# Attention scores from split float32r parts, and outputs gated where they are turned, in a two-layer hybrid block

## The reference, cut to what matters

```python
proj = h @ w_in[l]
q_a, kv_c, kv_s, kv_w, g_nsa, z_a, q_b, kv_b, z_b, merge = jnp.split(proj, pts, axis=-1)
kc = compress_blocks(...)                       # 31 compressed tokens
o_cmp, p_cmp = compressed_attention(qa, kc, vc, slopes_a)
o_slc = selected_attention(qa, ks, vs, blk_idx, slopes_a)
o_win = banded_attention(qa, kw, vw, slopes_a, NSA_WINDOW)       # 512
o_a = gts[0] * o_cmp + gts[1] * o_slc + gts[2] * o_win
y_a = (merge_heads(o_a) * jax.nn.silu(z_a)) @ w_o_nsa[l]
o_b = banded_attention(qb, kb, vb, slopes_b, SWA_WINDOW, sinks=sinks[l])   # 128
y_b = (merge_heads(o_b) * jax.nn.silu(z_b)) @ w_o_swa[l]
# in each of them: s = einsum(q, k) * dh ** -0.5, ALiBi, softmax, einsum(p, v); dh = 64
y = (jax.nn.sigmoid(m_a) * y_a + jax.nn.sigmoid(m_b) * y_b) @ w_out[l]
```

## Time and profile before

| | |
|---|---|
| runs | 1763.94, 1768.17, 1769.01 us; median 1768.17 |
| profiled execution | 1767.28 us, its span 1765.6 us |
| instructions | 28455 |
| busy | PE 95%, PE weight loads 86%, DVE 43%, POOL 34%, ACT 31% of the span |
| chain that ended last | issue 40%, PE 38%, POOL 17%, DVE 4%, ACT 1% |
| DMA | 141 MB, 80 GB/s on average |
| mean granted TensorE clock | 0.969 |

### The profile page before, as it was taken

The page is one execution under the profiler, slowest core; times in us unless marked ns, Lnnn a source line. Parts: engine busy times, 40 slices in busy tenths (PEclk is TensorE's granted clock), DMA queues, the critical chain, the costliest instruction groups (busy, mean ns, idle before and its releaser), DMA issues.

```text
span 1765.6 us, 28455 instructions
## 1 busy us (share of the span) xinstructions
PE 1668.9 (95%) x11374; PEld 1520.6 (86%) x11374; DVE 764.2 (43%) x1617; ACT 541.4 (31%) x870; POOL 605.7 (34%) x485
## 2 busy tenths in 40 slices
PE   5898999999989999999999999899999999999996
PEld 5676777777767799999999999899899899998996
DVE  5705555555566743323333311424622632371355
ACT  2323333333333432233322222323332242232222
POOL 3453222221225324444333444232442243233323
PEclk9999999999999889999999999899999999999998
DMA  8132111111124212222222222121121122212111
GB/s 323 72 120 83 46 40 46 47 48 48 48 96 167 96 49 95 95 75 92 74 92 95 95 76 92 49 75 69 64 81 72 49 73 72 72 50 74 70 49 72
DMA packets 22774, 141.15 MB, mean 80 GB/s; under 512 B 3248, under 2 KB 3248, under 8 KB 6448
## 3 DMA queue, kind: packets, MB, share of 16 engines
q1 hardware_dynamic: 18752, 131.08, 20.6%
q10 hardware_dynamic: 3952, 9.00, 1.4%
HBM read 137.98 MB, written 2.10 MB: 79 GB/s over the span
## 4 chain that ended last, share of the span: by engine, by line
issue 40%; PE 38%; POOL 17%; DVE 4%; ACT 1%; POOLq 0%; DVEq 0%; ACTq 0%
PE lin L365 31%; POOL w_lo L311 17%; PE aux L789 4%; PE aux L754 2%; DVE mix L1472 1%; PE aux L738 1%; PE aux L436 1%; DVE squares L1491 0%; DVE v_T L1492 0%; PE aux L393 0%; DVE residual L1511 0%; DVE tmp L1407 0%; PE aux L711 0%; PE aux L741 0%; ACT mix L1024 0%
## 5 line engine op out<-in xcount | busy, mean ns | idle before, releaser
L311 POOL TENSOR_TENSOR w_lo<-w_raw,w_hi 128x512 fp32r<-128x512 f32 x460 | 601.9, 1340 | 1141.8 <-ACT w_hi L353 1141.8
L365 PE MATMUL lin<-x_hi,w_hi 128*128 128x256 f32 (+2 forms) x2448 | 595.5, 311 | 32.7 <-POOL w_lo L311 16.9
L365 PE MATMUL lin<-x_lo,w_hi 128*128 128x256 f32 (+2 forms) x2448 | 584.1, 307 | 0.0
L365 PE MATMUL lin<-x_hi,w_lo 128*128 128x256 f32 (+2 forms) x2448 | 582.8, 306 | 0.0
L365 PEld LDWEIGHTS lin<-x_hi,w_hi 128*128 128x128 f32 x2448 | 396.9, 192 | 66.2 <-issue 24.5
L365 PEld LDWEIGHTS lin<-x_hi,w_lo 128*128 128x128 f32 x2448 | 396.7, 191 | 18.8
L365 PEld LDWEIGHTS lin<-x_lo,w_hi 128*128 128x128 f32 x2448 | 396.7, 191 | 14.8
L353 ACT ACTIVATE w_hi<-w_raw 128x2048 fp32r<-128x2048 f32 x115 | 219.4, 1908 | 158.1 <-PE lin L365 152.6
L861 ACT ACTIVATE prob<-prob,neg_max 128x31 f32<-128x31 f32 (+6 forms) x128 | 60.1, 471 | 157.5 <-DVE neg_max L1201 157.5
L1322 DVE TENSOR_TENSOR conv_in<-conv_c_gate,lin 128x272 f32<-128x272 f32 (+1 forms) x32 | 12.3, 427 | 213.8 <-PE lin L365 213.8
L365 PE MATMUL lin<-mix,w_hi 128*128 128x272 f32 (+1 forms) x512 | 84.7, 287 | 10.0 <-DVE mix L1472 7.1
(11 more groups left out here) (294 smaller groups left out, 2005.4 us busy)
## 6 DMA issues: line engine op xcount, KB each, us to landing
w_raw<-wstream SPq DMA_DIRECT2D x115, 1024.0 KB, 4.8
ada_shift_scale<-w_ada SPq DMA_DIRECT2D x8, 1024.0 KB, 19.0
ada_gate<-w_ada_gate ACTq DMA_DIRECT2D x4, 1024.0 KB, 5.9
residual<-x_t SPq DMA_DIRECT2D x1, 2048.0 KB, 8.7
residual<-x_t ACTq DMA_DIRECT2D x1, 2048.0 KB, 8.4
out_t<-residual ACTq DMA_DIRECT2D x8, 256.0 KB, 2.1
small_inputs<-smalls ACTq DMA_DIRECT2D x1, 537.0 KB, 3.4
residual<-meta_t ACTq DMA_DIRECT2D x1, 64.0 KB, 11.1
```

Of the source, the lines that this page charges most:

```text
L311: ins = eng.tensor_tensor(wlo[h][:, cols], raw[h][:, cols], whi[h][:, cols].bitcast(F32), ALU.subtract)
L365: ins = t.matmul(o, w[half][:, c0:c0 + P], x(k, t0, cnt), start=(n == 0), stop=(n == 3 * kts - 1))
```

## The change

Keys and queries are kept as a high float32r part and a low rest. The high keys lie twice, once on each half of the lanes, for each head; a head's queries lie with the high part on its own 64 lanes and the low part on the other 64. A score product is then two float32r matmuls: over 128 lanes, both parts of the queries by the high keys; and over 64 lanes, high queries by low keys. The compressed keys get a 32nd column of zeros. ACT writes the high parts (keys: four copies of 64 lanes; queries: two), DVE the low ones (two of 64 lanes). The scores of the next pair's first step go ahead of the last turn of a pair. The turned outputs are multiplied by z at once, in place in `zz`; behind the loop only the split is left, in an order that leaves the last pair to the end, and the first chunk's four tiles run together, input block by input block, two of them in other banks.

The core of the diff:

```diff
-        K_C, V_C, K_S, V_S, K_W, V_W, Q_B, K_B, V_B = 4, 5, 6, 7, 8, 9, 10, 14, 15
+        V_S, V_W, V_B = range(3)
+        K_S, K_W, K_B = range(3)
...
-            with eng.bass.Fori(0, NPAIR, 1, engines=[eng.engine]) as ii:
-                def scores(s):
...
-                    qa = proj[lo:hi, K_C, P * i:P * i + P]
-                    qb = proj[lo:hi, V_C, P * i:P * i + P]
-                    eng.matmul(b[0][:, 0:keys], qa, proj[lo:hi, K_S, 0:keys], start=True, stop=True)
-                    eng.matmul(b[1][:, 0:keys], qa, proj[lo:hi, K_W, 0:keys], start=True, stop=True)
-                    eng.matmul(b[2][:, 0:NC], qa, kct[lo:hi, e * NC:(e + 1) * NC], start=True, stop=True)
-                    w0 = 32 + (P if i == 0 else 0)
-                    eng.matmul(b[2][:, w0:w0 + keys - k0], qb, proj[lo:hi, K_B, k0:keys], start=True,
-                               stop=True).then_inc(s_scored, 1)
-
+            def scores(s, ii):
+                i, e = divmod(s, 2)
+                lo, hi = PAIR[e]
+                b = att_banks(e)
+                keys, k0 = P * (i + 1), max(0, P * (i - 1))
+                eng.wait_ge(s_o, ii * 8 + (s - 1 + CREDIT))
+                if e == 0:
+                    eng.wait_ge(s_oT_out, ii * 4 + (i - 1 + CREDIT))
+                if s == 0:
+                    eng.wait_ge(s_q, ii * 2 + 2)
+                if s == 1:
+                    eng.wait_ge(s_oT_out, ii * 4 + CREDIT)
+                qs = slice(P * i, P * i + P)
+                w0 = 32 + (P if i == 0 else 0)
+                for out, x, twice, low in (
+                        (b[0][:, 0:keys], 0, k_hi[:, K_S, e, 0:keys], k_lo[lo:hi, K_S, 0:keys]),
+                        (b[1][:, 0:keys], 0, k_hi[:, K_W, e, 0:keys], k_lo[lo:hi, K_W, 0:keys]),
+                        (b[2][:, 0:NC + 1], 0, kct_hi[:, e, :], kct_lo[lo:hi, e, :]),
+                        (b[2][:, w0:w0 + keys - k0], 1, k_hi[:, K_B, e, k0:keys], k_lo[lo:hi, K_B, k0:keys])):
+                    eng.matmul(out, q_parts[:, x, e, qs], twice, start=True, stop=False)
+                    ins = eng.matmul(out, q_parts[lo:hi, x, e, qs], low, start=False, stop=True)
+                ins.then_inc(s_scored, 1)
+
+            def pair(ii, last):
...
+                if not last:
+                    scores(0, ii + 1)
                 turn_outputs(QT - 1)
 
-            eng.wait_ge(s_tile_out, 6 * NPAIR + CREDIT)
-            for c in range(N_WO):
+            scores(0, 0)
+            with eng.bass.Fori(0, NPAIR - 1, 1, engines=[eng.engine]) as ii:
+                pair(ii, False)
+            pair(NPAIR - 1, True)
+
+            eng.wait_ge(s_tile_out, 4 * NPAIR)
+            eng.wait_ge(s_q, 2 * NPAIR + 2)
+            def wo_tile(c, m, x, ks=None):
+                return group(eng, c % 2, x * 1024 + m * P, 256, 4, [(wo_bank(2 * c + m, x)[:], TB1[0])],
+                             lambda k, t0, n: x_hi(4 * x + k, t0, n), lambda k, t0, n: x_lo(4 * x + k, t0, n), ks)
+
+            chunk_ready(START["wo"])
+            for n, k in enumerate(OG_ORDER):
+                eng.wait_ge(s_og_lo, n + 1)
+                for m in range(2):
+                    ins = wo_tile(0, m, k // 4, ks=[k % 4])
+                    if k % 4 == 3:
+                        ins.then_inc(s_chunk if m and k == KD - 1 else s_wo, 1)
+            for c in range(1, N_WO):
                 chunk_ready(START["wo"] + c)
                 for m in range(2):
                     for x in range(2):
                         j = 4 * c + 2 * m + x
-                        if j >= 2:
+                        if c > 1 or m:
                             eng.wait_ge(s_wo_out, j - 1)
-                        ins = group(eng, c % 2, x * 1024 + m * P, 256, 4, lin_outs(x, TB1),
-                                    lambda k, t0, n, x=x: x_hi(4 * x + k, t0, n), lambda k, t0, n, x=x: x_lo(4 * x + k, t0, n),
-                                    before=(lambda k, x=x: eng.wait_ge(s_og_lo, 4 * x + k + 1)) if j < 2 else None)
-                        ins.then_inc(s_chunk if m and x else s_wo, 1)
+                        else:
+                            eng.wait_ge(s_wo_out, x + 1)
+                        wo_tile(c, m, x).then_inc(s_chunk if m and x else s_wo, 1)
...
+            def query_high_parts(g):
+                for e, (p0, p1) in enumerate(PAIR):
+                    ins = act(q_parts[p0:p1, g, e, :], lin[g][p0:p1, 0, :], ACT.Copy, scale=DH ** -0.5)
+                ins.then_inc(s_qhi, 1)
+
             for c in range(N_PROJ):
                 chunk_lands_and_splits(eng, START["proj"] + c + 1)
                 if c in (1, 2):
                     eng.wait_ge(s_cin, c)
                     act(cin_hi[c - 1][:], cin[:], ACT.Copy).then_inc(s_cin_hi, 1)
+                if c in KEYS:
+                    eng.wait_ge(s_proj, PROJ_ORDER.index(c) + 1)
+                    for e, (p0, p1) in enumerate(PAIR):
+                        for half in range(2):
+                            ins = act(k_hi[half * DH:(half + 1) * DH, KEYS[c], e, :], lin[0][p0:p1, 0, :], ACT.Copy)
+                    ins.then_inc(s_khi, 1)
                 if c == 6:
-                    eng.wait_ge(s_cin, 2)
                     for g in range(2):
                         if g == 0:
                             eng.wait_ge(s_proj, 4)
                         else:
                             eng.wait_ge(s_chunk, START["proj"] + 6)
-                        act(proj[:, Q_HEADS + g, :], lin[g][:, 0, 0:T1], ACT.Copy, scale=DH ** -0.5).then_inc(s_q, 1)
+                        query_high_parts(g)
...
-            for k in range(KD):
-                eng.wait_ge(s_og, k + 1)
-                act(xhi[:, k, 0:T1], tmp[:, k % 2, 0:T1], ACT.Copy).then_inc(s_og_hi, 1)
+            eng.wait_ge(s_chunk, START["wo"])
+            for k in OG_ORDER:
+                x, pr = divmod(k, NPAIR)
+                eng.wait_ge(s_oT_out, 4 * (NPAIR if pr == NPAIR - 1 else NPAIR - 1) + CREDIT)
+                act(xhi[:, k, 0:T1], zz[:, x, pr, :], ACT.Copy).then_inc(s_og_hi, 1)
...
-                    copy(proj[:, CHUNK_TILE[c] + g, :], lin[g][:, 0, :]).then_inc(s_proj_out, 1)
+                    if g == 0 and c in KEYS:
+                        eng.wait_ge(s_khi, KEYS[c] + 1)
+                        for e, (p0, p1) in enumerate(PAIR):
+                            ins = tt(k_lo[p0:p1, KEYS[c], :], lin[0][p0:p1, 0, :], k_hi[p0:p1, KEYS[c], e, :].bitcast(F32), ALU.subtract)
+                    else:
+                        ins = copy(values[:, VALUES[c], :] if c else cmp_kv[:, g, :], lin[g][:, 0, :])
+                    ins.then_inc(s_proj_out, 1)
                     if g == 0 and between:
                         between()
+
+            def query_low_parts(g, at):
+
+                eng.wait_ge(s_qhi, at)
+                for e, (p0, p1) in enumerate(PAIR):
+                    o0, o1 = PAIR[1 - e]
+                    ins = stt(q_parts[o0:o1, g, e, :], lin[g][p0:p1, 0, :], DH ** -0.5, q_parts[p0:p1, g, e, :].bitcast(F32),
+                              ALU.mult, ALU.subtract)
+                ins.then_inc(s_q, 1)
...
+            for g in range(2):
+                query_low_parts(g, g + 1)
             hidden_turned(0)
             eng.wait_ge(s_cmp, 1)
-            ts(kct[:], aux[1][:, 0:2 * NC], 0.5, None, ALU.mult).then_inc(s_cmp_out, 1)
+            kc_raw = aux[1][:, 0:2 * NC].rearrange("p (g j) -> p g j", g=2)
+            for part in (kct_hi, kct_lo):
+                own.up(ts(part[:, :, NC:NC + 1], ones[:, 0:2].unsqueeze(2), 0.0, None, ALU.mult))
+            own.up(ts(kct_hi[:, :, 0:NC], kc_raw, 0.5, None, ALU.mult))
+            own.settle()
+            stt(kct_lo[:, :, 0:NC], kc_raw, 0.5, kct_hi[:, :, 0:NC].bitcast(F32), ALU.mult, ALU.subtract).then_inc(s_cmp_out, 1)
...
+                    if i == 0:
+                        eng.wait_ge(s_z_out, ii * 2 + 2)
                     for x in range(2):
-                        ins = move(flat(proj[:, bass.ds(ii + Q_B * x, 1), P * i:P * i + P]), turn_bank(i)[:, P * x:P * x + P])
+                        z = flat(zz[:, x, bass.ds(ii, 1), P * i:P * i + P])
+                        ins = stt(z, z, 0.5, turn_bank(i)[:, P * x:P * x + P], ALU.mult, ALU.mult)
                     ins.then_inc(s_oT_out, 1)
...
+                    if s >= 6:
+                        query_low_parts(s - 6, ii * 2 + (s - 3))
...
             def low_og(k):
                 eng.wait_ge(s_og_hi, k + 1)
-                tt(xlo[:, k, 0:T1], tmp[:, k % 2, 0:T1], xhi[:, k, 0:T1].bitcast(F32), ALU.subtract).then_inc(s_og_lo, 1)
+                x, pr = divmod(OG_ORDER[k], NPAIR)
+                tt(xlo[:, OG_ORDER[k], 0:T1], zz[:, x, pr, :], xhi[:, OG_ORDER[k], 0:T1].bitcast(F32), ALU.subtract).then_inc(s_og_lo, 1)
             for k in range(KD):
-                x, pr = divmod(k, NPAIR)
-                if k >= 2:
-                    eng.wait_ge(s_og_lo, k - 1)
```

(46 more changed lines are left out.)

24 lines of the change are left out of this document (5 added, 19 removed).

## The result

The kernel after takes 1785.95 us (median of four runs, 1781.85 to 1791.46), the kernel before 1768.59 beside it (1763.94 to 1772.48). The ratio is 1.0105, 95% interval [1.0076, 1.0134]: 17.4 us slower by the medians, where 1784.6 was forecast, +17.3. The profiled execution is the fastest of the four, 1781.85 us; its span is 1780.1.

The account below looks back on a forecast made before the run. TensorE (PE) was taken to bound the kernel, busy 95% of the span. The terms 0.9 + 3.2 + 2.5 + 4.0 + 1.6 + 8.0 - 2.9 gave +17.3, 1784.6 us; range 1749 to 1798, the forecast's own 1775 to 1795.

Parts of the forecast that it names:

- Keys ahead of the split: Projection chunk 1: ACT's four half-height key copies come ahead of its next split, which POOL and PE await: +0.9 us.
- Chunk 8: Last projection chunk: PE waits between tiles for key copies and tanh, +3.2 us; low clock for the second tile, +2.5.
- Scores: Attention loop's score steps: streaming per column halves, but eight changes of lanes a step cost 0.19 us each: +4.0 us.
- Rivals (1) and (2): Score products: 64-lane weight loads hide behind 128-lane matmuls, 1750.5 us (chance 0.22); or partly hidden, about 0.11, 1767 (0.09).
- Border chain: Borders between pairs: ACT reads tile 7 with two half-height copies, 0.53 us more, delaying split and transposes: +1.6 us for three.
- Clock at the borders: Pair borders: PE stands about 4.3 us before the transposes, then low clock covers work that binds: 2.7 three times, +8.0 us.
- rival (4): Clock also falls inside the steps, because PE streams less there: with three falls 1794.5 us, more with more; chance 0.13.
- Rival (3): Clock stays up at the borders and in chunk 8, since scores(0) fills today's gap: 1774 us; chance 0.12.
- Behind the loop: Output projections: gating already done in the turn's evacuation, so PE starts earlier and chunk 1's split is ready: -2.9 us.

Follow-up runs that it names:

- the run with the scores behind the turn: Kernel after the change, with the next pair's first scores issued behind the pair's last turn again, as before the change: 1788.48 us, ratio 1.0072 to the kernel before.
- the two runs on the order: Kernel after, score products grouped by lanes: 1767.79 us, ratio 0.9953; and low products replaced by high ones over 128 lanes, computation partly left out: 1760.20 us, 0.9912.
- two changes of lanes: Kernel after, with each step's eight score products reordered so lanes change twice, not eight times: 1767.79 us, ratio 0.9953 to the kernel before.
- the tanh alone: Kernel after, with only the compression's tanh put ahead of the keys' four copies in projection chunk 8: 1794.10 us, ratio 1.0103 to the kernel before.
- the version with two changes and the standing closed: Kernel after, with grouped score products, DVE's scalar copies early and maxima(0) ahead of the last turned outputs: 1741.88 us, ratio 0.9835 to the kernel before.
- the scalars early: Kernel after with grouped score products, and DVE's copies of the next pair's scalars moved ahead of the last PV: 1747.21 us, ratio 0.9854 to the kernel before.

## Why the prediction was right

The sign came out, and so did the mechanism of the scores, the term that decides. That the sum was met within 0.1 us is luck: the terms add up to 19.4 in the profiles, not 17.3, the story of one of them was wrong, and 4.9 us came back in code that the change doesn't touch. Offsets are starts after minus starts before of the same instruction.

- **Keys ahead of the split**, +0.9: the matmul at 79.89 comes at 80.79. Right.
- **Chunk 8**, +3.2 and +2.5: PE waits for 3.34 us. The low clock behind lasted only 3.4 us, 137.8 to 141.3, so +1.7. The loop's first projection matmul is at +6.1 (forecast 6.6).
- **Scores**, +4.0: measured +6.5: 1.85, 1.62 and 1.84 for the last three pairs by the run with the scores behind the turn, 1.2 for the first in the profile of after. The mechanism is right, the prices of the steps were low by 0.08 (i = 0) and 0.14 (i = 3). Above streaming, 128-column products lie 0.20 apart and 512-column products 0.21, where the forecast added 0.19. Taking changes away gives back 0.15 to 0.18 each, less, because products of equal lanes don't come at bare streaming either (0.11 and 0.23, not 0.05 and 0.21). Rivals (1) and (2) fall with the two runs on the order. That rule of the Trainium skill by which the loads could be hidden (TensorE: Matmul & The Clock Gate, Part 2, the LDWEIGHTS step) would have given 1750.5. No row here shows a load hidden across a change of lanes; between equal lanes the trace agrees with the rule.
- **Border chain**, +1.6: from the turn of step 6 to the transposes +0.88, +0.78 and +0.80, so +2.5. ACT's two half-height copies take 1.20 us, the single one took 0.60: 0.6 and not 0.53. From their start to POOL's it is 3.20 us, 2.47 before; the small rest lies behind POOL.
- **Clock at the borders**, +8.0: measured 29.44 us from the first border's transposes to the next turn, 26.51 where the second stretch is missing: +2.9, +2.9 and +1.5, together 7.3. Here the size was right and the story was not. The step that failed reads "PE does scores(0), the turn and the half group at full clock, and then stands for about 4.3 us". PE fell to 1.2 GHz during these scores, still had most of a low stretch in cover, stood for 1.5 us, and then a second one came. The forecast's own picture is to be seen only with two changes of lanes (4.7 us of standing, low behind it). The forecast also let the fall come 1.3 to 3.5 us into the standing, and no row of its shows the 3.5; in that run it came 5.2, 2.2 and 2.6 us behind the start of the standing at the three borders. So the part of rival (4) by which scores with eight changes behind PV bring the clock down fits scores(0) at the border. The second stretches begin during the scores of step 1; in no other step did the clock fall. Rival (3) is refuted.
- **Behind the loop**, -2.9: from the last turn (503.08 and 525.45, +22.4) to the first matmul of the next stage (567.65 and 587.09, +19.4), -2.9. Right.

The terms add up to 19.4 there. The profiled executions end 14.5 apart: 4.9 us come back in code that the change does not touch. PE's wait of 4.20 us at 1594.40 in the profile of before is one of 2.02 at 1610.32 in that of after, and the low stretches are shorter. That part varies from run to run: from the first matmul of the next stage to the end it is 1198 us before, 1193 after and 1203 to 1208 in the profiles of the nine later runs. It goes with the clock: its low stretches, without the one at the very end, add up to 44 us after (1193), 51 before (1198) and 58 to 65 later (1203 to 1208). What sets their number is open. The sum of 17.3 met the medians' 17.4 also because of that.

## What to carry to other kernels

- Halving the columns of the products bought nothing here, because each product changed the lanes of the array (the same time at i = 3, 0.67 us more at i = 0). Count the changes, price them from the pitch of rows on both sides of one, and group the products by lanes first: the order alone was worth 27 us, and turned a loss of 1.0% into a gain of 0.5%.
- Where a tuned loop has its low clock under cover, time saved ahead of it can come back as standing and a new low stretch (the tanh alone: 4.6 us gained at the loop's start, 1.2 left at its end). On the version with two changes and the standing closed, the same edit gave 5 us.
- Work without a deadline (ten copies of scalars) belongs in an engine's idle time ahead of the critical chain, not in it.

## What the hardware showed that was not expected

- A change of lanes costs PE 0.15 to 0.19 us at full clock, also beside a 512-column matmul, whose pitch of 0.23 us is longer than the load of 0.19 us. The load then begins only with its own product; between equal lanes it begins with the product before.
- The clock fell during eight score products with eight changes of lanes behind PV without a gap ahead of them (240.2 after); with two changes they run at a pitch of 0.11 to 0.16 and the clock stays at full behind them (232.8 to 240.9).
- Standing does not set it alone: 1.5 us ahead of the transposes was followed by a low stretch after, 1.3 us with the scalars early was not, at any of three borders. The two runs differ also in the scores behind the transposes (eight changes and two) and in the low stretch ahead of the standing, which only after has. Which of these tells them apart is open; eight changes with hardly any standing (0.25 to 0.51 us, the run with the scores behind the turn) were not followed by one either.
- Three copies of 128x4 on DVE took 0.30 us with POOL idle, 1.19 (after) and 2.37 (two changes) beside POOL's w_lo, and were done only when POOL's last piece had ended (244.70 and 244.53 after, 237.05 and 237.01 with two changes); the copies of 128x1 took 0.14 to 0.16 in either case.
